# Two pairs by seven products between plain ones in the FFN's first GEMM, and another order of splits at query projection and attention

## The chip, the core and the metric

The kernel runs on one core of one Trainium2 chip. The metric is the device time of one execution in microseconds. The time of the kernel before is 2525.53 us, the median of 3 runs (2525.16 to 2525.58).

## The reference

A decoder trunk of two layers on 1024 tokens with 16 learned tokens ahead of them (1040 columns), width 1024, in float32. Layer 0 is a Mamba-2 mixer and an FFN. Layer 1 is grouped-query attention in a window of 128 tokens, with a sink logit for each head, and an FFN. What matters here is the FFN, and query projection and attention:

```python
def conv_ffn(hn, w_up, conv_w, conv_b, w_down):
    u = causal_dwconv(hn @ w_up, conv_w, conv_b)      # (1040, 2 * 2816), 3 taps
    gate, val = u[..., :D_FF], u[..., D_FF:]
    return (jax.nn.silu(gate) * val) @ w_down

q = (hn @ w_q).reshape(bsz, seq_len, N_KV_HEADS, Q_PER_KV, ATTN_HEAD_DIM) * scale
p = softmax(concatenate([s_meta, s_band, s_sink], -1))
return concatenate([om, ob], axis=1) @ w_o
```

## The kernel before

Activations lie with features on the partitions and the 1040 columns (blocks of 272, 384 and 384) along the free side. Each float32 operand of a GEMM is split in two float16 parts, high and low, and a product is three matmuls: high by high, high by low, low by high. Weights come from memory by SyncE's queue into `stage` (two slots of one unit, a 128 x 1024 slice), in the order of the units: a unit is loaded when the low half of the unit two before it has been made (`w_lo`). ScalarE makes the high half (`hi`, `split_hi`, L884), VectorE the low half (`lo`, `split_lo`, L1594). Each engine works through a list of its own in program order and waits on semaphores.

**The FFN's first GEMM** (`ffn_up` of each engine) goes through 22 pairs, gate tile and value tile i. A plain pair is two tiles of 3 blocks x 8 k x 3 matmuls, 144 in all. ScalarE takes each tile from PSUM to `UB` and makes the first tap of the convolution, VectorE the other two (`conv_tile`, L2094), ScalarE the gate's SiLU (L1412), VectorE the product of both (`product`, L2102), ScalarE the high part of the hidden tile (L1416) and GpSimd its low part (`hidden_lo`, L791).

From pair 7 on every second pair, 8 of the 15 pairs 7 to 21, is computed by seven products of half-size blocks in place of eight (`seven_pair`, a Strassen-Winograd scheme): tokens, k and the two tiles are each cut in two. The seven weight operands are A11, A12, A22 as loaded and the sums S1 to S4, made from `stage` by GpSimd (`weight_sums`, L803 to L810; S3 and S4 overwrite parts of `stage`, S1 and S2 use one buffer `tmp`). ScalarE makes the seven high halves (`op_high`, L1356), VectorE the low ones (`op_low`, L2026), in one set of buffers `OPS`. They stand in the plain pair ahead: four before its first convolution, three before its second. The low half of S4 is the last to read `stage`; with it `w_lo` counts two, and the loads of the next pair go out. TensorE (L2659 to L2661) multiplies in the order A11, S2, A12, S3, S1, A22, S4, each in two pieces of 272 and 248 columns (`e + q`, 14 groups of 12 matmuls, PSUM bank `(e + q) % 7`). VectorE adds the products up from PSUM into `UB` (`add`, L2053), counting `seven_v`; group 13 needs the bank that the addition (6, 0) frees. Between the additions it makes the low halves of the next plain pair (`lo_next`), then come the taps (L2042) and the product. TensorE's first matmul is at L2260 to L2262 for plain pairs; those behind a seven-product pair wait for `seven_v` counts (`after_seven`).

**Query projection and attention.** VectorE's list before query projection is `k_low`, `pre(3, block)` for three blocks (normalised input and its low part) and the low halves of the units U_Q to U_Q + 3, in the order U_Q, U_Q + 1, U_Q + 2 (inside `pre` of the second block), U_Q + 3. In the projection it evacuates 24 groups (L2183) and, at some of them, splits the next units up to U_O + 1, the second unit of the output projection. Then it prepares the sinks and runs the attention's chunks n = 0 to 39: `masked(n)` (L2204) after TensorE's `scores(n)`, ScalarE's `exps(n)` (L1539), VectorE's `denominators(n)` (L2211), GpSimd's normalisation (L869), TensorE's transposes (L2776, L2778) and values, and the split of the result (`out_hi` on ScalarE, `out_lo` L2226 on VectorE). The output projection waits for the last `out_lo`.

Of the kernel before, what the change touches and what calls it, by code (L numbers as in the profile page):

```python
# [5 lines left out]
P = 128  # L6
# [19 lines left out]
WS = 64.0  # L26
# [76 lines left out]
NS = (KF - SF + 1) // 2  # L103
HALF, KH = L // 2, KD // 2
A11, A12, A22, S1, S3, S2, S4 = range(7)
# [57 lines left out]
def program(nc, h0, wa, wd, wdt, prm, out):  # L163
# [4 lines left out]
    with ExitStack() as ctx:  # L168
# [74 lines left out]
        tmp = BIG[:, 21, 0:HP]  # L243

        def op_src(o):
            return (stage[:, 1, 0:HP], stage[:, 1, HP:2 * HP], stage[:, 0, HP:2 * HP], tmp, stage[:, 0, 0:HP], tmp,
                    stage[:, 1, HP:2 * HP])[o]

# [407 lines left out]
        def _(eng):  # L656
# [137 lines left out]
            def weight_sums(layer, m, i0, before):  # L794

                n = NS * layer + i0
                a11, a12, a21, a22 = stage[:, 1, 0:HP], stage[:, 1, HP:2 * HP], stage[:, 0, 0:HP], stage[:, 0, HP:2 * HP]
                eng.drain()
                for s_ in range(2):
                    eng.wait_ge(w_in[s_], m * 32 + 16 * ((U_UP[layer] + 2 * (SF + 2 * i0)) // 2 + 1))  # L800
                if n > 0:
                    eng.wait_ge(op_lo, m * 7 + (7 * (n - 1) + 6))
                eng.tensor_tensor(tmp, a21, a22, ALU.add).then_inc(op_sum, 1)  # L803
                eng.drain()
                eng.tensor_tensor(a21, a11, a21, ALU.subtract).then_inc(op_sum, 1)
                before()
                eng.wait_ge(op_lo, m * 7 + (7 * n + 4))
                eng.tensor_tensor(tmp, tmp, a11, ALU.subtract).then_inc(op_sum, 1)
                eng.drain()
                eng.tensor_tensor(a12, a12, tmp, ALU.subtract).then_inc(op_sum, 1)  # L810

            def ffn_up(layer):

                for t in range(SF - 2):
                    hidden_lo(layer, t)
                weight_sums(layer, 0, 0, lambda: hidden_lo(layer, SF - 2))
                hidden_lo(layer, SF - 1)
                with eng.Fori(0, NS - 1) as m:
                    weight_sums(layer, m, 1, lambda: hidden_lo(layer, m * 2 + SF))
                    hidden_lo(layer, m * 2 + (SF + 1))  # L820
                hidden_lo(layer, KF - 1)
# [55 lines left out]
        def _(eng):  # L877
# [466 lines left out]
            def op_high(layer, m, i0, o):  # L1344

                n = NS * layer + i0
                landed = m * 32 + 16 * ((U_UP[layer] + 2 * (SF + 2 * i0)) // 2 + 1)
                if o == A11:
                    eng.wait_ge(w_in[1], landed)
                    if i0 > 0:  # L1350
                        eng.wait_ge(seven, m * 14 + 14 * n)
                if o == A22:
                    eng.wait_ge(w_in[0], landed)
                if o >= S1:
                    eng.wait_ge(op_sum, m * 4 + (4 * n + o - S1 + 1))
# [4 lines left out]
            def up_tap(layer, m, i0, s_):  # L1360

                col = m * 16 + (C_F[layer] + 8 * (SF + 2 * i0) + 4 * s_)
# [4 lines left out]
            def seven_pair(layer, m, i0, c0, gate, hidden, split_next):  # L1367

                n, i = NS * layer + i0, m * 2 + (SF + 2 * i0)
                eng.wait_ge(conv[1], i + c0)  # L1370
                for q in range(2):
                    eng.wait_ge(seven, m * 14 + (14 * n + 1 + q))
                    eng.activation(up_out(layer, 1, q, False), PS[:, q, 0:piece(layer, q)[1]], ACT.Copy,
                                   scale=1.0 / WS).then_inc(seven_a, 1)
                split_next(0)
                split_next(1)
                eng.drain()
                eng.wait_ge(seven_v, m * 14 + (14 * n + 12))
                up_tap(layer, m, i0, 0)
                eng.drain()  # L1380
                eng.wait_ge(seven_v, m * 14 + (14 * n + 14))
                up_tap(layer, m, i0, 1)
                eng.drain()
                eng.sem_inc(evac, 6)
                gate(i)
                hidden(i)

            def ffn_up(layer, boundary_):
# [18 lines left out]
                def split(i, s_, width=KD * P):  # L1407
                    split_hi(i * 16 + units_loaded(u0 + s_ + 2, s_), s_, width)

# [51 lines left out]
                def last_plain(m, i0):  # L1461

                    i = m * 2 + (SF - 1 + 2 * i0)
                    for o in (A11, A12, A22, S1):
# [1429 lines left out]
```

## Time and profile before

| | |
|---|---|
| median of 3 runs | 2525.53 us |
| the profiled execution | 2525.95 us |
| its span, first to last instruction | 2524.2 us |
| mean granted clock of TensorE | 0.992 |
| TensorE, VectorE, ScalarE, GpSimd busy | 98%, 64%, 46%, 24% of the span |
| first GEMM of the FFN, layer 0 and layer 1 | to about 1240 and 2290 us |
| query projection, attention | about 1520 to 1614, 1614 to 1737 us |

Engines in the rows: PE is TensorE (PEld its weight load), DVE VectorE, ACT ScalarE, POOL GpSimd, SP SyncE. A timeline row has start and duration in us, engine and line, operation, output<-input by the program's names, shape and count; in brackets stands the idle time of the engine just before it and what ended it. Matmuls overlap, so their starts tell the pace, and their durations do not.

### The profile page before, as it was taken

The numbers are of one execution on the slowest core, as the hardware profiler recorded it, in microseconds if no ns is written. First come the engines' busy times: TensorE is split into PE (matmuls) and PEld (weight loads), VectorE is DVE, ScalarE is ACT, GpSimd is POOL, SyncE is SP. The second block draws the span as 40 slices with busy tenths as digits, with TensorE's granted clock in tenths as the row PEclk, the third lists the DMA queues.
The fourth block names the chain that finished last, engine by engine and source line by source line (L and its number), as shares of the span: only waits on it lengthen the run. The fifth ranks groups of instructions, "written<-read, shape, count | busy, mean of one in ns | idle before, by whom it ended". The sixth has DMA issues, their size and how long they took to land.

```text
span 2524.2 us, 45974 instructions
## 1 busy us (share of the span) xinstructions
PE 2470.5 (98%) x18254; PEld 1724.5 (68%) x18254; DVE 1615.6 (64%) x2424; ACT 1155.4 (46%) x2166; POOL 602.3 (24%) x417
## 2 busy tenths in 40 slices
PE   8999999999999999999999999899999999999998
PEld 5566666666665667777766666676656777777665
DVE  6676777787868887777511276594379777772123
ACT  5455655666415554444311255595355444441111
POOL 1002113122142122232122113264411223221221
PEclk9999999999999999999999999999999999999999
DMA  3132222323132111212311112100121121213111
GB/s 118 54 104 79 85 84 80 97 68 99 45 127 101 51 51 50 65 35 66 126 46 58 40 34 68 34 2 18 43 110 50 51 66 34 66 56 126 46 57 67
DMA packets 67808, 167.69 MB, mean 66 GB/s; under 512 B 5680, under 2 KB 37840, under 8 KB 67408
## 3 DMA queue, kind: packets, MB, share of 16 engines
q1 hardware_dynamic: 67664, 165.70, 19.8%
q8 instruction: 99, 1.62, 0.3%
q14 instruction: 45, 0.37, 0.0%
HBM read 151.76 MB, written 12.86 MB: 65 GB/s over the span
## 4 chain that ended last, share of the span: by engine, by line
PE 86%; DVE 8%; ACT 3%; ACTq 1%; POOL 1%; issue 1%; DVEq 1%; DMA 0%
PE PS L2260 22%; PE PS L2262 22%; PE PS L2261 22%; PE PS L2661 4%; PE PS L2659 4%; PE PS L2660 4%; PE PS L2536 1%; PE PS L2543 1%; DVE BIG L1629 1%; PE PS L2525 1%; DVE TT L1693 1%; POOL BIG L869 1%; PE PS L2354 1%; ACT BIG L1539 1%; DVE R L460 1%
## 5 line engine op out<-in xcount | busy, mean ns | idle before, releaser
L2260 PE MATMUL PS<-R,whi 128*128 128x384 f16 (+2 forms) x2400 | 747.4, 311 | 2.6 <-DVE wlo L1594 1.6
L2262 PE MATMUL PS<-R,wlo 128*128 128x384 f16 (+2 forms) x2400 | 747.2, 311 | 0.0
L2261 PE MATMUL PS<-R,whi 128*128 128x384 f16 (+2 forms) x2400 | 747.1, 311 | 0.0
L1594 DVE SCALAR_TENSOR_TENSOR wlo<-stage,whi 128x1024 f16<-128x1024 f32 (+1 forms) x148 | 204.5, 1383 | 380.7 <-ACT whi L884 379.9
L2260 PE MATMUL PS<-BIG,whi 128*128 128x384 f16 (+2 forms) x1404 | 435.4, 310 | 4.9 <-DVE wlo L1594 4.2
L2262 PE MATMUL PS<-BIG,wlo 128*128 128x384 f16 (+2 forms) x1404 | 435.4, 310 | 0.0
L2261 PE MATMUL PS<-BIG,whi 128*128 128x384 f16 (+2 forms) x1404 | 435.3, 310 | 0.0
L2260 PEld LDWEIGHTS PS<-R,whi 128*128 128x128 f16 x2400 | 235.3, 98 | 127.7 <-issue 14.2
L2261 PEld LDWEIGHTS PS<-R,whi 128*128 128x128 f16 x2400 | 235.4, 98 | 121.3 <-issue 9.8
L2262 PEld LDWEIGHTS PS<-R,wlo 128*128 128x128 f16 x2400 | 235.4, 98 | 118.0 <-issue 1.0
L884 ACT ACTIVATE whi<-stage 128x1024 f16<-128x1024 f32 (+1 forms) x148 | 162.5, 1111 | 148.3 <-PE PS L2262 128.5
L791 POOL TENSOR_TENSOR BIG<-TT,BIG 128x1040 f32 (+3 forms) x44 | 95.4, 2168 | 462.4 <-ACT BIG L1416 462.4
L2094 DVE SCALAR_TENSOR_TENSOR TT<-UB,pr,TT 128x1040 f32<-128x1040 f32 (+1 forms) x104 | 161.6, 1554 | 59.6 <-ACT TT L1421 46.8
L2260 PEld LDWEIGHTS PS<-BIG,whi 128*128 128x128 f16 x1404 | 137.2, 98 | 76.4 <-issue 6.5
L2261 PEld LDWEIGHTS PS<-BIG,whi 128*128 128x128 f16 x1404 | 137.2, 98 | 68.7 <-issue 2.6
L2262 PEld LDWEIGHTS PS<-BIG,wlo 128*128 128x128 f16 x1404 | 137.2, 98 | 68.0
L748 POOL TENSOR_TENSOR TT<-R 128x384 f32<-128x384 f32 (+2 forms) x63 | 51.5, 832 | 400.6 <-ACT R L897 261.6
L2659 PE MATMUL PS<-hT,AUX 128*128 128x272 f16 (+3 forms) x512 | 140.1, 274 | 0.0
L2661 PE MATMUL PS<-hT,AUX 128*128 128x272 f16 (+3 forms) x512 | 140.0, 274 | 0.0
L2660 PE MATMUL PS<-hT,AUX 128*128 128x272 f16 (+3 forms) x512 | 139.9, 273 | 0.0
L1693 DVE SCALAR_TENSOR_TENSOR TT<-UB,pr,TT 128x1040 f32<-128x1040 f32 x72 | 102.4, 1422 | 46.9 <-ACT TT L994 42.9
L1416 ACT ACTIVATE BIG<-TT 128x1040 f32 (+3 forms) x44 | 46.8, 1064 | 180.2 <-DVE TT L2102 180.2
(285 smaller groups left out, 4556.7 us busy)
## 6 DMA issues: line engine op xcount, KB each, us to landing
stage<-wa SPq DMA_DIRECT2D x164, 512.0 KB, 3.5
stage<-wd SPq DMA_DIRECT2D x32, 704.0 KB, 4.0
TT<-cs_rows SPq DMA_DIRECT2D x32, 512.0 KB, 3.7
h_keep<-hT SPq DMA_DIRECT2D x2, 4160.0 KB, 12.4
EC<-cs_rows SPq DMA_DIRECT2D x64, 128.0 KB, 3.7
hT<-h SPq DMA_DIRECT2D x4, 1536.0 KB, 10.6
hT<-h_keep SPq DMA_DIRECT2D x4, 1536.0 KB, 8.5
out<-hT SPq DMA_DIRECT2D x4, 768.0 KB, 3.5
```

Of the source, the lines that this page charges most:

```text
L748: eng.tensor_tensor(T1[:, s:s + n], cut(mix(m, b), b, lo_), cut(mix(m, b), b, lo_), ALU.mult)
L791: eng.tensor_tensor(BIGh[:, ds(t, 1), L + a:2 * L], T2[:, a:], BIGh[:, ds(t, 1), a:L], ALU.subtract).then_inc(hid_lo, 1)
L884: eng.activation(WH[slot + 2 * aux][:, 0:width], stage[:, slot, 0:width], ACT.Copy, scale=WS).then_inc(w_hi, 1)
L1594: eng.scalar_tensor_tensor(out=WL[d][:, 0:width], in0=stage[:, slot, 0:width], scalar=WS, in1=WH[d][:, 0:width], op0=ALU.mult, op1=ALU.sub ...
L1693: r = eng.scalar_tensor_tensor(out=T0, in0=UB[:, i % 2, o:o + L], scalar=prc(C_AW + (g * GT + j) * CONV_A + k), in1=T0, op0=ALU.mult, op1= ...
L2094: r = eng.scalar_tensor_tensor(out=dst, in0=cin[:, o + ld_:o + L], scalar=prc(col + k), in1=dst, op0=ALU.mult, op1=ALU.add)
L2260: eng.matmul(acc, WH[slot][:, ws], xh, start=first, stop=False)
L2261: eng.matmul(acc, WH[slot][:, ws], xl, start=False, stop=False)
L2262: return eng.matmul(acc, WL[slot][:, ws], xh, start=False, stop=last)
L2659: eng.matmul(acc, ops[o][:, w], moving(0, kk, q), start=(kk == 0), stop=False)
L2660: eng.matmul(acc, ops[o][:, w], moving(1, kk, q), start=False, stop=False)
L2661: r = eng.matmul(acc, ops[7 + o][:, w], moving(0, kk, q), start=False, stop=(kk == KH - 1))
```

## The change

The stretch from pair 7 on gets another pattern: a seven-product pair 7, then four turns of one plain pair and two seven-product pairs (8, 9, 10; 11, 12, 13; 14, 15, 16; 17, 18, 19), then plain 20 and seven-product 21. That makes 10 seven-product pairs in place of 8. The operands are numbered in TensorE's order, S2 gets a buffer of its own (`tmp2`). The operands of the second of two adjacent pairs are made inside the first: ScalarE's high halves ahead of its taps, S4's between them; VectorE's low halves A11, S2, A12, S3 between the additions and S1 behind the taps; A22 and S4 inside the second pair itself. ScalarE's copies of a pair's first product (`seven_first`) move ahead of the hidden tile of the pair before. At query projection the low halves of U_Q + 1 to U_Q + 3 and the high halves of U_Q + 2 and U_Q + 3 move ahead of `pre` and `split_x` of the second block; the sinks are prepared ahead of the projection's evacuations; `masked(0)` moves ahead of the last evacuation; the halves of U_O + 1 move from the end of the projection to the third last chunk of attention.

```diff
-NS = (KF - SF + 1) // 2
+RS = 2
+RP = RS + 1
+NR = (KF - SF - 3) // RP
+NS = 2 + RS * NR
-A11, A12, A22, S1, S3, S2, S4 = range(7)
+A11, S2, A12, S3, S1, A22, S4 = range(7)
+FIRST, REST = (A11, S2, A12, S3), (S1, A22, S4)
...
@@ GpSimd: weight_sums @@
                 eng.tensor_tensor(tmp, a21, a22, ALU.add).then_inc(op_sum, 1)
                 eng.drain()
+                eng.tensor_tensor(tmp2, tmp, a11, ALU.subtract).then_inc(op_sum, 1)
                 eng.tensor_tensor(a21, a11, a21, ALU.subtract).then_inc(op_sum, 1)
+                eng.drain()
                 before()
-                eng.wait_ge(op_lo, m * 7 + (7 * n + 4))
-                eng.tensor_tensor(tmp, tmp, a11, ALU.subtract).then_inc(op_sum, 1)
-                eng.drain()
-                eng.tensor_tensor(a12, a12, tmp, ALU.subtract).then_inc(op_sum, 1)
+                eng.wait_ge(op_lo, m * (7 * RS) + (7 * n + A12 + 1))
+                eng.tensor_tensor(a12, a12, tmp2, ALU.subtract).then_inc(op_sum, 1)
...
@@ ScalarE: op_high, seven_pair @@
+                if beside:
+                    eng.wait_ge(seven, m * (14 * RS) + (14 * (n - 1) + 2 * o + 2))
...
+                if op_next is not None:
+                    for o in FIRST + REST[:-1]:
+                        op_next(o)
                 eng.drain()
+                eng.wait_ge(seven_v, m * (14 * RS) + (14 * n + 12))
+                up_tap(layer, m, i, 0)
+                if op_next is not None:
+                    op_next(S4)
...
-                gate(i)
-                hidden(i)
+                gate(i_)
+                if op_next is not None:
+                    seven_first(layer, m, i + 1, n0 + 1, c0)
+                hidden(i_)
...
@@ VectorE: seven_pair @@
                     add(2, q, u2[q], c11[q])
+                if op_own is not None:
+                    op_own(A22)
                 eng.drain()
                 for q in range(2):
                     add(4, q, c11[q], c11[q])
-                lo_next(0)
+                if op_own is not None:
+                    op_own(S4)
+                if lo_next is not None:
+                    lo_next(0)
+                ops(A11, S2)
                 for q in range(2):
                     add(6, q, u3[q], u2[q])
-                lo_next(1)
+                if lo_next is not None:
+                    lo_next(1)
+                ops(A12, S3)
                 for q in range(2):
                     add(8, q, u4[q], u2[q])
...
+                ops(S1)
+                product(m * RP + i)
...
@@ VectorE: ffn_up @@
-                with eng.Fori(0, NS - 1) as m:
-                    seven_pair(layer, m, 0, product, lambda s_: split_lo(m * 4 + (u0 + 2 * SF + 3 + s_), s_))
-                    last_plain(m, 1)
+                with eng.Fori(0, NR) as m:
+                    last_plain(m, SF + 1, 1, SF)
+                    for j in range(RS - 1):
+                        seven_pair(layer, m, SF + 2 + j, 1 + j, product, op_next=lambda o: op_low(layer, m, 2 + j, o),
+                                   op_own=(lambda o: op_low(layer, m, 1 + j, o)) if j else None)
+                    seven_pair(layer, m, SF + RP, RS, product, lo_plain(m, SF + RP + 1),
+                               op_own=lambda o: op_low(layer, m, RS, o))
...
@@ VectorE: query projection and attention @@
             pre(3, ORD[0], lambda: lo(U_Q, aux=True))
+            lo(U_Q + 1, aux=True)
             k_low(ORD[2])
-            lo(U_Q + 1, aux=True)
-            pre(3, ORD[1], lambda: lo(U_Q + 2))
+            lo(U_Q + 2)
             lo(U_Q + 3)
+            pre(3, ORD[1])
             pre(3, ORD[2])
...
+                if c == len(Q_SEQ) - 1:
+                    masked(0)
...
+                if q_next(i, b) and i < KD - 1:
+                    lo(U_Q + i + 2)
...
                 if n + 2 < NQD:
                     masked(n + 2)
+                if n + 3 == NQD:
+                    lo(U_O + 1)
...
@@ TensorE: seven_pair @@
+                def free(bank):
+                    if behind_seven:
+                        eng.wait_ge(seven_v, m * (14 * RS) + (14 * (n - 1) + (6, 10, 12, 12, 12, 13)[bank]))
+                    else:
+                        eng.wait_ge(evac, m * (6 * RP) + (kept + bank + 1))
...
+                if behind_seven:
+                    eng.wait_ge(seven_v, m * (14 * RS) + 14 * n)
```

## Rows read from the trace of the kernel before

**Rows 1.** the page: busy us of each engine, share of the span, instructions:

```profile
PE 2470.5 (98%) x18254; PEld 1724.5 (68%) x18254; DVE 1615.6 (64%) x2424; ACT 1155.4 (46%) x2166; POOL 602.3 (24%) x417
```

**Rows 2.** TensorE's waits: us in total, times, longest:

```profile
PE PS L2760 <- DVE small L2204: 4.6, 2, 4.4
```

**Rows 3.** windows, layer 0: busy us of PE, PEld, DVE, ACT, POOL, then clock:

```profile
1040.00:1080.00 40.00, 40.00 (x316) 30.60 (x314) 29.34 (x34) 18.11 (x26) 11.03 (x6) 1.00 0.16 52
```

**Rows 4.** TensorE's timeline (start, us): seven products begin, end, next ones begin:

```profile
1056.80 0.28 PE L2659 MATMUL PS<-R,AUX 128*128 128x272 f16 x1
...
1075.42 0.28 PE L2260 MATMUL PS<-R,whi 128*128 128x272 f16 x1
...
1096.58 0.28 PE L2659 MATMUL PS<-R,AUX 128*128 128x272 f16 x1
```

**Rows 5.** VectorE's timeline in that stage:

```profile
1045.78 2.43 DVE L2026 SCALAR_TENSOR_TENSOR AUX<-stage,AUX 128x512 f16<-128x512 f32 x1 [1.76 <-ACT AUX L1356]
...
1050.32 2.14 DVE L2094 SCALAR_TENSOR_TENSOR TT<-UB,pr,TT 128x1040 f32<-128x1040 f32 x1 [0.30 <-issue]
...
1055.82 0.68 DVE L2026 SCALAR_TENSOR_TENSOR AUX<-stage,AUX 128x512 f16<-128x512 f32 x1
...
1066.60 1.42 DVE L1594 SCALAR_TENSOR_TENSOR wlo<-stage,whi 128x1024 f16<-128x1024 f32 x1
1068.62 1.21 DVE L1594 SCALAR_TENSOR_TENSOR wlo<-stage,whi 128x1024 f16<-128x1024 f32 x1
...
1077.55 1.70 DVE L2042 SCALAR_TENSOR_TENSOR TT<-UB,pr,TT 128x1040 f32<-128x1040 f32 x1 [0.20 <-issue]
...
1082.46 1.24 DVE L2102 TENSOR_TENSOR TT<-TT 128x1040 f32<-128x1040 f32 x1 [0.23 <-issue]
```

**Rows 6.** ScalarE's timeline: two high halves of the next plain pair:

```profile
1065.00 2.00 ACT L884 ACTIVATE whi<-stage 128x1024 f16<-128x1024 f32 x2
```

**Rows 7.** GpSimd's timeline in that stage:

```profile
1045.51 2.16 POOL L791 TENSOR_TENSOR BIG<-TT,BIG 128x1040 f32 x1 [7.04 <-ACT BIG L1416]
...
1051.53 2.07 POOL L810 TENSOR_TENSOR stage<-stage,BIG 128x512 f32<-128x512 f32 x1 [0.16 <-issue]
```

**Rows 8.** SyncE's timeline, then loads of 1054 to 1078, us to landing:

```profile
1056.72 0.86 SPq L613 DMA_DIRECT2D stage<-wa  x2
...
stage<-wa SPq DMA_DIRECT2D x4, 512.0 KB, 4.0
```

**Rows 9.** a wait of TensorE, then windows behind it, columns as Rows 3:

```profile
PE PS L2556 <- DVE BIG L1707: 4.1, 1, 4.1
...
107.00:108.00 1.00, 0.00 (x0) 0.00 (x0) 1.00 (x2) 1.00 (x5) 0.00 (x0) 0.50 0.00 0
...
113.00:114.00 1.00, 1.00 (x7) 0.43 (x6) 0.08 (x1) 0.45 (x1) 0.00 (x0) 0.72 0.01 4
```

**Rows 10.** VectorE's timeline before and at query projection:

```profile
1530.75 1.21 DVE L1594 SCALAR_TENSOR_TENSOR wlo<-stage,whi 128x1024 f16<-128x1024 f32 x1
...
1535.68 1.23 DVE L1594 SCALAR_TENSOR_TENSOR wlo<-stage,whi 128x1024 f16<-128x1024 f32 x1 [0.39 <-ACT whi L884]
...
1543.93 5.74 DVE L2183 SCALAR_TENSOR_TENSOR BIG<-PS,BIG 64x384 f16<-64x384 f32 x10 [0.34 <-ACT BIG L1526]
```

**Rows 11.** timelines of VectorE and TensorE at the start of attention:

```profile
1616.29 1.23 DVE L1594 SCALAR_TENSOR_TENSOR wlo<-stage,whi 128x1024 f16<-128x1024 f32 x1
...
1619.38 0.35 PE L2760 MATMUL PS<-BIG 128*112 128x128 f16 x1 [4.41 <-DVE small L2204]
```

**Rows 12.** timelines at attention's end: ScalarE, VectorE, TensorE twice:

```profile
1730.62 0.19 ACT L1539 ACTIVATION_READ_ACCUMULATOR BIG<-BIG,small 32x1 f32 x1
...
1728.60 0.17 DVE L2211 RECIPROCAL small<-small 32x4 f32<-32x4 f32 x1
...
1732.40 0.31 PE L2776 MATMUL PS<-ident,BIG 32*128 32x32 f32 x1 [0.57 <-POOL BIG L869]
...
1737.45 0.40 PE L2260 MATMUL PS<-R,whi 128*128 128x260 f16 x1 [0.98 <-DVE R L2226]
```

More of the change, by code:

```diff
@@ L792, in hidden_lo, with weight_sums @@
                                   ALU.subtract).then_inc(hid_lo, 1)
[L794 to L796 removed]
+            def weight_sums(layer, m, i, n, before):
+                n += NS * layer
                 a11, a12, a21, a22 = stage[:, 1, 0:HP], stage[:, 1, HP:2 * HP], stage[:, 0, 0:HP], stage[:, 0, HP:2 * HP]
@@ L1565, in _ @@
                     exps(n + 2)
+                if n + 3 == NQD:
+                    hi(U_O + 1)
                 if n > 0:
@@ L2045, in up_taps, with seven_pair @@
                     r.then_inc(conv[s_], 1)
-            def seven_pair(layer, m, i0, product, lo_next):
-                n, i = NS * layer + i0, m * 2 + (SF + 2 * i0)
+            def seven_pair(layer, m, i, n, product, lo_next=None, op_next=None, op_own=None):
+                n0, n = n, NS * layer + n
                 def add(e, q, dst, term):
-                    eng.wait_ge(seven, m * 14 + (14 * n + e + q + 1))
+                    eng.wait_ge(seven, m * (14 * RS) + (14 * n + e + q + 1))
                     eng.scalar_tensor_tensor(out=dst, in0=PS[:, (e + q) % 7, 0:piece(layer, q)[1]],
@@ L2055, in add, with ops @@
                                              op0=ALU.mult, op1=ALU.add).then_inc(seven_v, 1)
+                def ops(*os):
+                    if op_next is not None:
+                        for o in os:
+                            op_next(o)
                 c11, c12 = ([up_out(layer, 1, q, r) for q in range(2)] for r in (False, True))
@@ L2227, in out_lo @@
                 r.then_inc(out_lo_ready, 1)
-            masked(0)
+            for c, (i, b) in enumerate(Q_SEQ):
+                s, n = BLK[b]
+                if c == len(Q_SEQ) - 1:
+                    masked(0)
+                eng.wait_ge(kq_hi, 6 + c + 1)
+                for hh in range(2):
+                    own, other = slice(64 * hh, 64 * hh + 64), slice(64 - 64 * hh, 128 - 64 * hh)
+                    q_ = q_stack(2 * i + hh, s, s + n)
+                    r = eng.scalar_tensor_tensor(out=q_[other], in0=PS[own, c % 6, 0:n],
+                                                 scalar=1.0 / (WS * AD ** 0.5), in1=q_[own],
+                                                 op0=ALU.mult, op1=ALU.subtract)
+                r.then_inc(evac, 1)
+                if q_next(i, b) and i < KD - 1:
+                    lo(U_Q + i + 2)
             masked(1)
```

209 lines of the change are left out of this document (108 added, 101 removed).

## The prediction

> **What bounds the kernel now.** I read the profile in this order: the busy line [rows 1], the waits of TensorE [rows 2], one of the two stages of the FFN's first GEMM by windows [rows 3], then one settled loop pass of that GEMM engine by engine [rows 4 to 8], and last the three places around query projection and attention [rows 9 to 12]. TensorE is busy for 98% of the span, and in the FFN stage a window of 40 us holds 40.00 us of matmuls at full clock [rows 3]. The other layer's stage looks the same, and no wait of TensorE in either is listed. So there only fewer columns help. The reader is to see two things more. VectorE works 29.3 of the 40 us there [rows 3], which looks like a quarter in reserve; but it and ScalarE hand the same tile to and fro, so the reserve is made of waits. And the profiled run took 2525.95 us, its span 2524.2; the median of the runs is 2525.53, so I add differences of spans to the median.
>
> **FFN, what is saved.** A pair by seven products starts at 1056.80 and ends at 1075.42: 18.62 us. The plain pair behind it ends at 1096.58: 21.16 us [rows 4]. Before there are 8 of the 15 pairs behind pair 6 by seven products, afterwards 10 (7, then 9 and 10, 12 and 13, 15 and 16, 18 and 19, then 21). Two pairs a layer: 2 x 2.54 = 5.1 us, for both layers 10.2 us, if TensorE never waits.
>
> **FFN, what is added: a load behind the second pair.** Call the two adjacent pairs A and B. The plain pair P behind B can be loaded into `stage` only when the last low half of B (S4) has been made, because S4 is read from `stage`. Before, S4 was made in the plain pair ahead, its last low ended at 1056.5 [rows 5], the loads went out at 1056.72 [rows 8] while A began, and P's low halves were made at 1066.60 and 1068.62 [rows 5], long before 1075.42. In the new order VectorE makes S4 of B inside B, and the very next item in its queue is the low half of P (`lo_next(0)`). So VectorE stands still for load, ScalarE's high half and its own low half, and behind it in the queue are the additions of products 6 to 13, with the one (6,0) that frees the bank of TensorE's last product but for it. Its length: issue 0.2, landing 4.4 (4.0 is the median of four such loads [rows 8], and of two that go out together the second is the later one), high half 1.0 [rows 6], hand-over 0.2: 5.8 us idle (its lower bound, with a load of 3.5, is 4.9). Then 1.14 low and 0.4 addition: 7.5 us from S4's end to TensorE's go.
>
> TensorE reaches that wait 17.3 us into B (18.62 less the last 1.3). No stall therefore needs S4 of B at B + 9.8. When can it be there? With a VectorE that is never late A's product of gate and value starts 25.7 us into A, as at 1082.46, and takes 1.24 [rows 5]. With low S1 (0.6) and the first part of B (two additions, A22, two additions, S4: 3.0) that is A + 30.5, or B + 11.9; one port wait (below) of 0.6 makes it B + 12.5. 12.5 + 7.5 - 17.3 = 2.7, and I take 3.0 us of stall for the first of the four turns of each layer.
>
> **FFN, how the lag grows.** In the later turns VectorE starts late, since it lost those 5.8 us. I add up its queue over one turn P, A, B, in the order of the changed code: idle for the load 5.8; two low halves of P and the additions of B 6.4; idle for a tap 1.2; taps, last addition and product of B 7.5; idle for ScalarE (hidden tile, then A11's high half) 1.8, the idle time at 1045.78 [rows 5]; seven low halves of 0.61, two tile convolutions of 2 x 1.30, two idles for taps (0.5 and 2.1) and a product: 13.8; A's additions and four lows of B 8.1; idle for a tap 1.2; taps 6.3, S1 0.6, product 1.3; B's first part 3.0. Sum 57.0 us. TensorE's own turn is 21.16 + 2 x 18.62 = 58.4 us. So far VectorE would just keep up.
>
> What decides is the port between VectorE and GpSimd. A low half of 512 columns takes 0.68 us [rows 5], but the one issued at 1045.78 took 2.43: GpSimd's subtraction ran until 1047.67, and it ended 0.5 us behind that [rows 5, 7]. GpSimd's sum of 512 columns at 1051.53 took 2.07 us beside a tap, others of its shape 1.3, so it goes both ways. The additions from PSUM are not touched. In the pass from 1040 to 1080 VectorE loses 4.2 us so: 1.75 at 1045.78, 0.84 and 0.75 at the taps of 1050.32 (2.14 for 1.30) and behind it, 0.2 at 1066.60 (1.42 for 1.21), 0.2 and 0.4 at the taps before and at 1077.55 (1.70) [rows 5]. GpSimd ran six instructions then, 11.0 us [rows 3]. A turn of the new order has eleven of them (three hidden tiles, eight sums), 20 us. By proportion that is 7.6 us; laid beside VectorE's queue one by one I get 8.3 (A11 of A 1.6, S2 of B 2.0, S4 of B 1.0, six taps and products about 3.7). I take 8.3: a turn of 65.3 us. The bounds are 0 and 11 us. The Trainium skill ("SBUF — State Buffer", section "SBUF: two separate sides") says that this pair of ports is an exclusive lock, which a VectorE instruction with two SBUF inputs and a GpSimd one hold for their whole length; the trace agrees, with 2.43 us for 0.68. If the loss were a shared bandwidth instead, the sum would be nearer the 57.0.
>
> Per layer: layer 0: 3.0 + 3 x (65.3 - 58.4) = 23.7, less 5.1: +18.6 us. In layer 1 TensorE's tiles are 13 columns shorter and its turn 57.65 us: 3.3 + 3 x 7.65 - 5.05 = +21.2. Together **+39.8 us**. Moving ScalarE's copies of the first product ahead of the hidden tile gains VectorE 1.6 us at the start of A; that is in the sum. The first GEMM's other pairs and the second GEMM keep their order.
>
> **TensorE's clock.** After a wait of 4.1 us that began at 104.6, the granted clock was at 0.50 (1.2 GHz of 2.4) and came back only at about 113.3, 4.7 us of work later [rows 9]. Stalls of 5 us before B's last product can do the same: 2.3 us of TensorE time each. As VectorE is the later one in P anyway, I count 0 for them and keep 6 x 2.3 = 14 us for the range.
>
> **Query projection.** TensorE waits 4.5 us in all for low halves of units U_Q+1 to U_Q+3 (the last two made at 1530.75 and 1535.68 [rows 10]). Moved ahead, they are ready at 1523.7, 1526.7 and 1529.9 (the last waits for its load, issued at 1523.9, and its high half), so these waits go. But the two `pre` end 1.6 us later, and the first evacuation, which ran at 1543.93, comes at 1545.6 to 1546.8. The seventh group would now start at 1543.8 and needs that bank. So 3.0 of 4.5 us come back: gain 1.8 us (ends 0 and 4.5).
>
> **Start of attention.** TensorE waits 4.4 us for `masked(0)` [rows 2], behind an evacuation, the low half of U_O+1 (1616.29, 1.23 us) and the sinks [rows 11]. With `masked(0)` ahead of the last evacuation it ends at 1615.9 instead of 1619.3; the chain of scores, exponentials and normalisation that follows it is then bound by ScalarE and by GpSimd's copies of queries, about 0.4 us later than by the masking itself: gain 2.9 us (ends 0 and 4.4).
>
> **End of attention.** The high half of U_O+1 now stands behind ScalarE's last exponentials, which end at 1730.8 [rows 12], and its low half in VectorE's queue ahead of `denominators` of the last chunk but one. That reciprocal ran at 1728.60; it now waits until 1731.9 for the high half and 1.2 for the low one, to 1733.1. The last chunk's transposes, at 1732.40 before, start at 1736.0: 3.6 us later, and the output projection (1737.45) with them [rows 12]. Net of both: +0.7. Outside the FFN the sum is -1.1 us (from -7 to +4).
>
> Total: 39.8 - 1.1 = 38.7, so 2525.5 + 38.7 = **2564 us**.
>
> **Rivals.**
> 1. *The port costs little and VectorE keeps up.* For it: its queue sums to 57.0 against 58.4. Then only the load behind S4 counts, 0.4 to 3 us a turn, eight turns: -10.2 + 3 to 24 - 1 = -8 to +13, that is 2517 to 2539. It decides from a port loss under 1.4 us a turn. Against it is the row of 2.43 us, and that a turn has eight sums where a pass before had four.
> 2. *All is hidden.* S4 lands by B + 9.8 and the full 10.2 + 1 is gained: 2514 us, the other side. It needs VectorE 3 us quicker in a chain whose links all have rows; a ScalarE that runs taps earlier could do part of it.
> 3. *The stalls also halve the clock and TensorE becomes the late one in P.* Up to +14: 2570 to 2585. For it [rows 9], against it that VectorE has more to do in P than TensorE.
> 4. *The reordering beside attention goes wrong or the FFN does not change at all:* not likely, as the code is plain; part of the ranges.
>
> **How the numbers follow.** Forecast (turn of 62 to 67 us) 0.74; rival 1 0.12, of which a third is faster, a third about the same; rival 3 0.08; rival 2 0.06. About 0.2%, 5 us, is what a measurement here can tell from none. Slower: 0.74 + 0.08 + 0.04 = 0.86; same 0.04; faster 0.10. The range goes from the top of rival 1 to the upper end of rival 3: 2536 to 2584. The forecast alone spans 2548 to 2575.
>
> **What would show it.** TensorE's waits in the FFN: rows on VectorE's addition of `UB` of 3 us in the first turn and about 5 in the later ones, at the last group of each second pair; VectorE idle 5.8 us for `whi` once a turn; period of three pairs near 65 us; low halves of 2 us and more where GpSimd runs. In attention: the wait of 4.4 us gone, the last transposes later. I would be wrong if S4 of B ends before B + 10, or if those loads land in 3 us.

## The result and the profile after

The changed kernel takes 2563.1 us (median, 2559.5 to 2564.0) against 2525.6 us before: ratio 1.0143, 95% interval 1.0131 to 1.0156, 37.5 us slower. The profiled execution took 2562.72 us with a span of 2560.6; the span grew by 36.4 us, and the comparison below goes by spans. Forecast were 38.7.

The page's busy line (columns as [rows 1]) and TensorE's waits (as [rows 2]) of the kernel after:

```profile
PE 2478.6 (97%) x18350; PEld 1742.0 (68%) x18350; DVE 1658.1 (65%) x2500; ACT 1162.9 (45%) x2170; POOL 643.6 (25%) x433
...
PE PS L2727 <- DVE UB L2087: 26.3, 8, 4.1
...
PE PS L2850 <- POOL BIG L880: 8.0, 8, 5.0
...
PE PS L2321 <- DVE BIG L2283: 3.1, 1, 3.1
PE PS L2834 <- DVE small L2250: 3.0, 2, 2.0
```

No engine's share has moved by more than a point, yet a new row stands on top: a wait of 3.3 us on average, eight times, of a seven-product matmul (L2727) for VectorE's addition (L2087). In place of the wait of 4.4 us for the first mask [rows 2] stand two, of 1.0 and 2.0 us (last row); the last three rows are the places around attention, of which more below.

By the starts of TensorE's first matmul of each kind (as [rows 4]) the time divides so. From pair 7's start to the end of pair 21 the FFN of layer 0 took 297.08 us before and takes 312.57, that of layer 1 took 293.89 and takes 311.17: +15.5 and +17.3, so **+32.8** in the FFN. The stretch between the two FFN stages grew from 752.4 to 755.5 us, the rest of the span by 0.6: **+3.6** outside.

A turn is now a plain pair P and two seven-product pairs A and B. Its length, from one P to the next, is 61.5, 63.3, 65.1 and 64.0 us in layer 0 and 59.8, 64.9, 62.8 and 64.4 in layer 1; TensorE's own work in it is 58.4 and 57.8. One turn and what ends it, from the timelines of TensorE, VectorE, ScalarE and SyncE (SPq: issue of the loads); start, us, then the instruction, in brackets its idle time before:

```profile
1018.12 0.43 PE L2321 MATMUL PS<-R,whi 128*128 128x272 f16 x1
...
1080.08 0.28 PE L2727 MATMUL PS<-R,AUX 128*128 128x248 f16 x1 [3.83 <-DVE UB L2087]
...
1081.46 0.43 PE L2321 MATMUL PS<-R,whi 128*128 128x272 f16 x1
...
1071.58 2.01 DVE L2060 SCALAR_TENSOR_TENSOR AUX<-stage,AUX 128x512 f16<-128x512 f32 x1
1078.45 1.23 DVE L1629 SCALAR_TENSOR_TENSOR wlo<-stage,whi 128x1024 f16<-128x1024 f32 x1 [4.86 <-ACT whi L895]
1079.59 0.76 DVE L2087 SCALAR_TENSOR_TENSOR UB<-PS,UB 128x272 f32<-128x272 f32 x2
...
1077.36 1.06 ACT L895 ACTIVATE whi<-stage 128x1024 f16<-128x1024 f32 x1 [6.69 <-DMA stage<-wa]
...
1073.81 8.17 SPq L621 DMA_DIRECT2D stage<-wa  x4
```

Read it in the order of time: S4's low half (L2060) ends at 1073.59, the load is issued at 1073.81 and lands by 1077.36, the high half takes 1.06, VectorE has stood idle for 4.86 us, makes the low half (L1629), and only then comes the addition for which TensorE waits until 1080.08. In the kernel before the first of these low halves was made 8.8 us before the end of the seven-product pair, which takes 18.6 [rows 4, 5].

### The profile page after: what moved, and what is told of

It is laid out like the page before. It is cut to its first block, busy times and chain, and to the rows that moved or that the text cites. A ratio compares the mean times of both kernels' runs of the same rounds, so it can differ in the third digit from the quotient of the medians.

```text
span 2560.6 us, 46249 instructions
## 1 busy us (share of the span) xinstructions
PE 2478.6 (97%) x18350; PEld 1742.0 (68%) x18350; DVE 1658.1 (65%) x2500; ACT 1162.9 (45%) x2170; POOL 643.6 (25%) x433
## 4 chain that ended last, share of the span: by engine, by line
PE 72%; DVE 12%; DVEq 5%; ACT 4%; issue 3%; DMA 2%; POOL 1%; ACTq 1%; POOLq 0%; SPq 0%
PE PS L2321 19%; PE PS L2322 19%; PE PS L2323 19%; DMA stage<-wa 2%; DVE TT L2076 2%; PE PS L2727 2%; PE PS L2729 2%; PE PS L2728 2%; PE PS L2597 1%; PE PS L2604 1%; DVEq L2063 1%; DVE BIG L1664 1%; PE PS L2586 1%; DVE UB L2087 1%; DVE TT L1728 1%
## 5 line engine op out<-in xcount | busy, mean ns | idle before, releaser
L2321 PE MATMUL PS<-R,whi 128*128 128x384 f16 (+2 forms) x2208 | 690.3, 313 | 2.7 <-DVE wlo L1629 1.5
L2322 PE MATMUL PS<-R,whi 128*128 128x384 f16 (+2 forms) x2208 | 689.8, 312 | 0.0
L2323 PE MATMUL PS<-R,wlo 128*128 128x384 f16 (+2 forms) x2208 | 689.2, 312 | 0.0
L1629 DVE SCALAR_TENSOR_TENSOR wlo<-stage,whi 128x1024 f16<-128x1024 f32 (+1 forms) x140 | 193.4, 1383 | 423.3 <-ACT whi L895 422.5
L2321 PEld LDWEIGHTS PS<-R,whi 128*128 128x128 f16 x2208 | 218.2, 99 | 120.0 <-issue 14.4
L2322 PEld LDWEIGHTS PS<-R,whi 128*128 128x128 f16 x2208 | 218.0, 99 | 113.3 <-issue 9.6
L2323 PEld LDWEIGHTS PS<-R,wlo 128*128 128x128 f16 x2208 | 218.0, 99 | 109.7 <-issue 1.0
L895 ACT ACTIVATE whi<-stage 128x1024 f16<-128x1024 f32 (+1 forms) x140 | 155.5, 1115 | 208.8 <-PE PS L2323 129.7
L2727 PE MATMUL PS<-hT,AUX 128*128 128x272 f16 (+3 forms) x640 | 174.9, 273 | 1.2 <-ACT UB L1385 1.2
L2729 PE MATMUL PS<-hT,AUX 128*128 128x272 f16 (+3 forms) x640 | 174.7, 273 | 0.0
L2728 PE MATMUL PS<-hT,AUX 128*128 128x272 f16 (+3 forms) x640 | 174.6, 273 | 0.0
L2727 PE MATMUL PS<-R,AUX 128*128 128x272 f16 (+1 forms) x480 | 134.0, 279 | 26.3 <-DVE UB L2087 26.3
L2142 DVE SCALAR_TENSOR_TENSOR TT<-UB,pr,TT 128x1040 f32<-128x1040 f32 (+1 forms) x88 | 123.0, 1398 | 43.5 <-ACT TT L1448 33.1
L2076 DVE SCALAR_TENSOR_TENSOR TT<-UB,pr,TT 128x1040 f32<-128x1040 f32 (+1 forms) x80 | 122.4, 1531 | 33.4 <-ACT TT L1376 24.1
```

Of the source, the lines that this page charges most:

```text
L895: eng.activation(WH[slot + 2 * aux][:, 0:width], stage[:, slot, 0:width], ACT.Copy, scale=WS).then_inc(w_hi, 1)
L1629: eng.scalar_tensor_tensor(out=WL[d][:, 0:width], in0=stage[:, slot, 0:width], scalar=WS, in1=WH[d][:, 0:width], op0=ALU.mult, op1=ALU.sub ...
L2076: r = eng.scalar_tensor_tensor(out=dst, in0=UB[:, s_, o + a:o + L], scalar=prc(col + k), in1=dst, op0=ALU.mult, op1=ALU.add)
L2142: r = eng.scalar_tensor_tensor(out=dst, in0=cin[:, o + ld_:o + L], scalar=prc(col + k), in1=dst, op0=ALU.mult, op1=ALU.add)
L2321: eng.matmul(acc, WH[slot][:, ws], xh, start=first, stop=False)
L2322: eng.matmul(acc, WH[slot][:, ws], xl, start=False, stop=False)
```

## The experiments

**The parts apart.** The FFN's part alone (query projection and attention as before), and the other part alone (FFN as before). Of the first edit the core is shown, the second is its mirror:

```diff
# FFN alone: the order at projection and attention as before
-            lo(U_Q + 2)
-            lo(U_Q + 3)
-            pre(3, ORD[1])
+            pre(3, ORD[1], lambda: lo(U_Q + 2))
+            lo(U_Q + 3)
...
-                if n + 3 == NQD:
-                    lo(U_O + 1)
```

> The change without its parts at query projection and attention. By the traces of before and after, the stretch from pair 7 to pair 21 is 15.5 us longer in layer 0 and 17.3 us in layer 1, and the rest of the span 3.6 us longer. If the parts are independent: 2525.5 + 32.8 = 2558 to 2560 us, with TensorE's waits on additions of 2 to 4 us at the last product but for one group of each second pair. If the order at attention had fed back on layer 1's FFN, the 17.3 us of layer 1 would change.

> The other half of the change alone, the FFN as before. Theory: query projection loses 1.3 us (4.5 us of waits go, a wait of 3.1 comes for the seventh group's bank, and the granted clock falls to 0.50 behind it), the start of attention gains 2.7, its end loses 4.5: 3 us longer, 2528 to 2529 us. As predicted, without a fall of the clock, it would be 2524.5.

Measured: 2559.8 us (ratio 1.0133, interval 1.0116 to 1.0150) and 2528.0 us (1.0010, 1.0000 to 1.0019). The first has the eight waits on the addition, 26.8 us in all, and its two FFN stages take 312.3 and 311.8 us; the second has the FFN of before and its stretch between the stages is 2.6 us longer. So the FFN brings 34 of the 37.5 us. The other orders cost some 2 us rather than gain, a difference that only just clears the noise.

**One pair by seven products instead of two.** The changed kernel with its constant at one, and the single pair's low halves all made in the plain pair ahead:

```diff
-RS = 2
+RS = 1
...
-                               op_own=lambda o: op_low(layer, m, RS, o))
+                               op_own=(lambda o: op_low(layer, m, RS, o)) if RS > 1 else None)
```

> The whole change with its constant of two pairs set to one, so that pairs by seven products and plain pairs alternate one by one again, as in the kernel before, while the rest of the change (numbering, the other order of splits at query projection and attention) stands. Theory (only the second pair in a row has its load behind S4 in VectorE's queue): the FFN is that of the kernel before, and the time that of the kernel with the other order of splits alone, 2527 to 2530 us. Rival, something else in the new helper costs by itself: over 2535 us.

Measured: 2528.2 us (1.0007, 0.9997 to 1.0016), the same as the other orders alone. Neither the numbering of operands nor the helper costs by itself; it takes two adjacent pairs.

**VectorE's queue: the low halves of P later.** In pair B the two low halves of P, with the idle time ahead of them, are moved behind the additions for which TensorE waits:

```diff
                 if op_own is not None:
                     op_own(S4)
-                if lo_next is not None:
+                if lo_next is not None and op_own is None:
                     lo_next(0)
...
-                if lo_next is not None:
+                if lo_next is not None and op_own is None:
                     lo_next(1)
...
+                if lo_next is not None and op_own is not None:
+                    lo_next(0)
+                    lo_next(1)
                 add(12, 0, c12[0], u4[0])
```

> The changed kernel, but in the second pair of a turn VectorE makes the two low halves of the next plain pair behind the additions of products 8 to 11, so that no addition stands behind the load. Theory (VectorE's queue standing still for the load makes the wait and the lag): the waits on additions go, a wait of 2 to 3 us for the plain pair's low halves comes in their place at its start, both layers together some 20 us shorter, about 2541 us (2534 to 2548). Rival (VectorE has too much work in a turn, whatever its order, with GpSimd at its port): the time stays at 2558 to 2563 us.

**The other end of the same chain: A22 and S4 of B earlier**, between the taps of A's two tiles, so that `stage` is free earlier and the load is nearly done when VectorE asks for it (the line with `op_own(A22)` goes as well):

```diff
                 up_taps(layer, m, i, n0, 0, (0,))
+                ops(S1, A22, S4)
                 up_taps(layer, m, i, n0, 1, (1, 0))
-                ops(S1)
                 product(m * RP + i)
...
-                if op_own is not None:
-                    op_own(S4)
```

> The changed kernel, but VectorE makes the low halves S1, A22 and S4 of the second pair inside the first one, between the taps of its two tiles. The load of the plain pair then goes out some 10 us earlier, about 4 us into the second pair. Theory (S4's late low half and the load behind it): no wait at the last product but one; a wait of up to 3 us stays in the middle of the second pair for ScalarE's copies of its first product, as VectorE's taps come later. 25 to 35 us shorter, about 2531 us (2526 to 2538). Rival (too much work on VectorE and its port): at most a few us shorter, 2555 or more.

Measured: 2526.8 us (1.0007, 0.9997 to 1.0016) and 2526.6 us (1.0004, 0.9995 to 1.0014): either move takes back the whole loss. For the first that is more than expected: 2541 us, from 2534 to 2548, stood there, with a wait of 2 to 3 us on P's low halves, and about 1 us was left of it. The same low half with the idle time before it, from VectorE's timelines, first with the low halves later, then with S4 earlier:

```profile
1074.45 2.42 DVE L1629 SCALAR_TENSOR_TENSOR wlo<-stage,whi 128x1024 f16<-128x1024 f32 x2 [1.38 <-ACT whi L895]
```

```profile
1066.74 2.48 DVE L1629 SCALAR_TENSOR_TENSOR wlo<-stage,whi 128x1024 f16<-128x1024 f32 x1 [0.58 <-ACT whi L895]
```

The idle time of 4.86 us shrinks to 1.38 and 0.58, and no row on the additions is left. In layer 0 a turn is 59.0 to 60.0 us in the one and 58.4 to 59.7 in the other. What stays is one wait of about 1 us a turn, on P's low half (10.0 us in 11 waits over the whole kernel) in the first, on ScalarE's copy of B's first product (7.5 in 6) in the second. That is where most of the saving of 10.2 us goes in these two.

**The port.** GpSimd's sums of weights cut to 16 columns. All loads, waits and VectorE's work are kept; the two operands that had stood in `tmp` and `tmp2` are read from `stage` instead. The kernel leaves the sums out for all other columns, so its output is not the reference's:

```diff
-                eng.tensor_tensor(tmp, a21, a22, ALU.add).then_inc(op_sum, 1)
+                eng.tensor_tensor(tmp[:, 0:16], a21[:, 0:16], a22[:, 0:16], ALU.add).then_inc(op_sum, 1)
```

> The whole change, with GpSimd's part of a pair's weight sums cut to 16 of its columns (these sums are left out for all other columns, and products 5 and 6 of a pair take a block of the weights in place of the sum, so the output differs); instruction counts, loads, waits and VectorE's work stay. Theory of the prediction, as the runs so far leave it (the cost is VectorE's idle for the load; the lock of the port adds 8.3 us to VectorE's work in a turn): the idle stays, with the additions after it faster by up to some 2 us a turn; 8 stalls shrink from 3.3 to about 1.5 to 2 us, and less of the half clock follows, so 2543 to 2553 us. Rival, the port is nothing here: 2560 to 2566 us as the change. Rival, the port is all of it: 2526 us or less, and no wait on VectorE's additions left in the pairs.

Measured: 2533.8 us (1.0035, 1.0021 to 1.0048), below the range of the theory and above that of the port as the only cause. The eight stalls came out as expected, 1.5 to 2.0 us (13.9 in all); the range given with them did not follow from them: 2525.5 and 13.9, less the 10.2 saved, plus 2.6 outside the FFN, is 2531.8. Three turns of the changed kernel, then two of this one, columns as [rows 3]:

```profile
1018.12:1081.46 63.34, 59.51 (x483) 47.36 (x481) 48.24 (x58) 27.25 (x38) 21.50 (x11) 0.99 0.13 47
1081.46:1146.54 65.08, 61.31 (x482) 48.19 (x480) 49.82 (x63) 27.26 (x38) 20.82 (x11) 0.95 0.16 53
1146.54:1210.58 64.04, 61.20 (x481) 48.21 (x480) 48.92 (x60) 27.36 (x38) 21.17 (x11) 0.95 0.15 49
```

```profile
1015.38:1075.66 60.28, 58.58 (x483) 46.88 (x480) 45.30 (x60) 27.20 (x38) 10.83 (x11) 1.00 0.16 52
1075.66:1135.78 60.12, 58.58 (x483) 46.89 (x481) 45.29 (x60) 27.20 (x38) 10.64 (x11) 1.00 0.15 52
```

VectorE does the same instructions in 45.3 us instead of 48.2 to 49.8, and the turn falls from 64.2 us on average to 60.2. Its idle time, the turn less the busy time, hardly moves: 15.1 to 15.3 us before this edit and 14.8 to 15.0 with it, and the wait for `whi` is still 4.94 us. So it is VectorE's busy time that GpSimd stretches, not a later operand.

**Both taken away:** S4 early and the short sums together.

> The change with both suspected costs taken away at once: low S1, A22 and S4 of the second pair made inside the first, and GpSimd's sums cut to 16 columns (these sums are left out for all other columns, products 5 and 6 take a block of weights in their place, so the output differs). Theory (each of the two alone leaves VectorE's turn at 59.4 to 60.2 us against TensorE's 58.4): together they leave VectorE some 55 us, no wait of TensorE on VectorE's additions, and the full saving of 10 us in the two stages, less the 2.6 of the other order of splits: 2517 to 2520 us. Rival, the waits on ScalarE's copies come from their place in the queue alone and stay at about 1 us a turn: 2524 to 2527 us.

Measured: 2517.9 us (0.9969, 0.9957 to 0.9981), as the theory has it. No wait of TensorE over 0.2 us is left in the two stages, and they take 292.0 and 288.9 us, which is the sum of their pairs, 10.1 less than before. A turn of it:

```profile
1013.84:1072.24 58.40, 58.40 (x483) 46.97 (x480) 45.21 (x60) 27.09 (x38) 11.80 (x11) 1.00 0.17 55
```

Seen together, the cures do not add up: with the idle time gone the kernel gets 36 us faster than the change, with the sums gone 29, with both gone 45. A turn is 64 us long where TensorE's own work is 58.4; each of the two alone takes the turn to 59 to 60 us, and nothing can be gained below 58.4.

**Projection and attention.** The order of before and the new one mixed: the fourth query unit's low half inside the normalisation of the second block, the first mask early, the halves of the output unit (U_O + 1) behind the last chunk of attention. Once with the FFN of before, once with the FFN whose S4 is early:

```diff
             lo(U_Q + 2)
-            lo(U_Q + 3)
-            pre(3, ORD[1])
+            pre(3, ORD[1], lambda: lo(U_Q + 3))
...
-                if n + 3 == NQD:
-                    lo(U_O + 1)
...
             out_lo(NQD - 1)
+            lo(U_O + 1)
```

> The kernel before's FFN with the same order of splits in between the two at query projection and attention. Theory: waits of 4.5 us at the projection go, of which up to 2.3 come back at the seventh group without a fall of the clock, 2.7 at the start of attention are gained and nothing is lost at its end: 2520 to 2523 us. Rival, the stall at the seventh group stays, with the half clock behind it: 2526 to 2529 us.

> FFN as in the run with the second pair's low S1, A22 and S4 made inside the first pair (2526.6), and an order of splits at query projection and attention in between the two: the fourth query unit's low half inside the normalisation of the second block, its high halves around that unit, the first mask early as in the change, and the second unit of the output projection last, as before the change. Theory: in the run with the other order of splits alone, a wait of 3.1 us at the seventh group and the half clock behind it cost 6 us, and the end of attention 2; with the low half earlier inside the block's normalisation and the output unit put back, the gains of 1.8 to 2.9 at projection and 2.7 at the start of attention stand: 2519 to 2523 us. Rival, the stall at the seventh group stays, with its half clock: 2526 to 2529 us.

Measured: 2519.5 us (0.9972, 0.9963 to 0.9981) and 2518.7 us (0.9970, 0.9957 to 0.9982), both about half a microsecond or less below the ranges given. TensorE's waits tell why. Its timeline with this order and the FFN of before:

```profile
1547.83 0.34 PE L2263 MATMUL PS<-BIG,whi 128*128 128x384 f16 x1 [0.36 <-DVE BIG L2226]
```

The seventh group waits 0.36 us instead of 3.12, and the clock behind it stays at 1.00. At the start of attention the waits for the masks are 1.0 and 2.0 us, as in the change. The last two waits of the transposes for GpSimd are 0.7 and 0.4 us, where the changed kernel has one of 5.0, and the stretch between the FFN stages is 745.8 us, 6.6 less than before.

**A version that beats both.** On top of that low S1, A22 and S4 of B go behind A's last taps, so that ScalarE's copies for B start earlier, and P's low halves one step later:

```diff
-                ops(S1, A22, S4)
                 up_taps(layer, m, i, n0, 1, (1, 0))
+                ops(S1, A22, S4)
...
                 for q in range(2):
                     add(6, q, u3[q], u2[q])
+                if lo_next is not None and op_own is not None:
+                    lo_next(0)
...
                 for q in range(2):
                     add(8, q, u4[q], u2[q])
+                if lo_next is not None and op_own is not None:
+                    lo_next(1)
```

> The version with both mendings (2518.7 us) with two moves in the second pair: its low S1, A22 and S4 come behind the last taps of the first pair instead of between them, so that ScalarE's copies for the second pair start 2 us earlier, and the two low halves of the plain pair come one step later in VectorE's queue, behind the additions of products 6 and 7 and of 8 and 9. Theory: the waits of 0.8 to 1.5 us on ScalarE's copies, one a turn, are what eats most of the 10 us that two more pairs by seven products save; they go, and VectorE still finds its next high half ready to within 1 us: 2510 to 2515 us. Rival, VectorE with the port has no slack left for 58.4 us a turn whatever the order, and the waits only move to another row: 2517 to 2521 us.

Measured: **2512.7 us** (0.9947, 0.9933 to 0.9960), 12.8 us faster than before and 50 faster than the change. Its waits in the seven-product lines, and one turn:

```profile
PE PS L2725 <- DVE UB L2087: 1.1, 3, 0.4
...
PE PS L2725 <- ACT UB L1385: 0.3, 1, 0.3
...
1013.16:1071.56 58.40, 58.40 (x483) 46.91 (x480) 47.22 (x59) 27.31 (x38) 21.08 (x11) 1.00 0.16 53
```

With GpSimd's full 21.1 us of work in the turn VectorE gets by with 47.2 us, and TensorE is the bound again. The two stages take 292.9 and 290.4 us, which is 7.7 of the 10.2 us saved. So the port alone does not undo the change; it did so through an order that had no room for it. Which of the two moves brings how much was not run apart.

## Why the prediction was right, step by step

The mechanism in the FFN was right, and so was the size within a fifth. That the total came out within 1.2 us of the forecast is in part luck: the FFN was forecast 7.0 us too long (39.8 against 32.8) and the rest 4.7 us too short (-1.1 against +3.6), and the two misses nearly cancel.

**The saving.** 18.62 and 21.16 us for the two kinds of pair stand; the run without waits shows 10.1 of the 10.2 us.

**The load behind S4.** Right in kind and place, a little too long. Forecast were 5.8 us of idle VectorE, with 4.9 as the lower bound; 4.86 was measured, because the load landed in 3.55 us rather than the 4.4 taken from the median and a surcharge for the second of two. From S4's end to TensorE's go: 6.5 instead of 7.5 us. In the first turn S4's low half ended 13.1 us into B (forecast 12.5), and the stall was 2.1 us (2.7, rounded to 3.0).

**VectorE's turn.** Forecast 57.0 us of queue and 8.3 lost at the port, 65.3; measured 64.2 in layer 0 (63.3, 65.1, 64.0). The groups of VectorE's instructions over three turns (1018 to 1210; line, shapes, count, busy us, mean ns, idle before) let both terms be read:

```profile
L2076 DVE SCALAR_TENSOR_TENSOR TT<-UB,pr,TT 128x1040 f32<-128x1040 f32 x24 | 37.0, 1540 | 11.5 <-ACT TT L1376 8.3 <-issue 3.1
L2060 DVE SCALAR_TENSOR_TENSOR AUX<-stage,AUX 128x512 f16<-128x512 f32 x30 | 34.9, 1188 | 5.8 <-ACT AUX L1368 5.8
L2087 DVE SCALAR_TENSOR_TENSOR UB<-PS,UB 128x272 f32<-128x272 f32 x42 | 18.3, 435 | 2.5 <-issue 1.3 <-PE PS L2729 0.7
...
L2142 DVE SCALAR_TENSOR_TENSOR TT<-UB,pr,TT 128x1040 f32<-128x1040 f32 x12 | 17.4, 1448 | 8.0 <-ACT TT L1448 5.9 <-issue 2.1
...
L2060 DVE SCALAR_TENSOR_TENSOR AUX<-BIG,AUX 128x512 f16<-128x512 f32 x12 | 10.7, 894 | 0.4
L1629 DVE SCALAR_TENSOR_TENSOR wlo<-stage,whi 128x1024 f16<-128x1024 f32 x6 | 7.3, 1220 | 14.5 <-ACT whi L895 14.5
```

An undisturbed tap takes 1.30 us and a low half 0.68. The 36 taps are 7.6 us over that, the 42 low halves 17.0: 24.6 in three turns, **8.2 us a turn** where 8.3 were forecast. What is left of the turn is 56.0 against 57.0, and 0.9 of that difference is the shorter idle time for the load. One term of the 57.0 was added up wrongly: seven low halves of 0.61, the two convolutions, two idle times and a product make 13.3 us, and 13.8 was written. The additions, which read PSUM, keep their 0.44 us (435 ns), as the sum assumed. With the short sums the taps are back at 1301 ns, and in three turns (1015.38 to 1195.94) the 42 low halves take 41.2 us: 4.2 us of loss a turn, nearly all of it beside GpSimd's three hidden tiles, which were left whole. The Trainium skill ("SBUF — State Buffer", section "SBUF: two separate sides") says that whichever of the two starts first holds the pair of ports for its whole instruction, while the other waits. The rows agree: S4's low half takes 2.01 us where a GpSimd instruction of 2.17 us had begun 0.7 us before it, in one turn after the other.

**The sum over the turns.** Over TensorE's own work the first turn of layer 0 was 3.1 us longer, the other three 17.3 together, the last plain pair 0.2: less 5.1 that is +15.5, against 18.6. In layer 1 it was 2.0 + 18.9 + 1.4 - 5.0 = +17.3, against 21.2. The miss is in the main the 1.1 us a turn just named, and in layer 1 also a first stall that was 1.5 us shorter than taken.

**The clock.** The prediction counted nothing for a halved clock in the FFN, since VectorE is the later one in P. The clock did fall behind the long stalls, as windows of the changed kernel show around a stall of 3.77 us that ends at 1144.09:

```profile
1141.00:1142.00 1.00, 0.00 (x0) 0.00 (x0) 0.00 (x0) 0.64 (x1) 0.00 (x0) 1.00 0.95 389
...
1143.00:1144.00 1.00, 0.00 (x0) 0.00 (x0) 1.00 (x3) 0.66 (x1) 0.00 (x0) 0.50 0.00 0
...
1148.00:1149.00 1.00, 1.00 (x6) 0.66 (x5) 0.47 (x2) 0.70 (x1) 0.00 (x0) 0.50 0.93 348
1149.00:1150.00 1.00, 1.00 (x9) 0.74 (x7) 0.29 (x1) 0.56 (x1) 0.00 (x0) 0.74 0.13 53
```

TensorE loses some 2.7 us by it (5 us at 0.50, 1.2 GHz, and a window at 0.74). Yet the turn is hardly longer for it. In the run with the short sums the clock stayed at 1.00, and VectorE's idle time in a turn was 14.8 to 15.0 us; here it is 15.1 to 15.3, and no more than 0.3 us of it in a turn ends with a matmul. The rest of the difference between the turns, 3.7 of 4.0 us, is VectorE's busy time. So the slow matmuls fill time that would have been a longer stall. That is why the waits read 3.8 us and not the "about 5" that the prediction said a reader would find. Rival 3 saw the fall rightly and its price wrongly. Not covered by VectorE are only the first turn of layer 0 (3.1 us longer with a stall of 2.1, so 1.0) and the last plain pair of each stage (0.2 and 1.4).

**Outside the FFN** the forecast was -1.1, and +3.0 was measured between the stages, +3.6 in all. The step that failed is the projection, forecast as a gain of 1.8 us and measured as a loss of 1.3. Its mechanism held: the waits of 4.5 us went, and the seventh group waited 3.12 us for its bank (3.0 forecast). But this stall halved the clock as well, which the prediction had counted for the FFN's range and not here. Windows of the changed kernel:

```profile
1561.00:1563.00 2.00, 0.00 (x0) 0.00 (x0) 0.85 (x2) 1.93 (x5) 1.55 (x7) 0.88 0.02 8
1563.00:1565.00 2.00, 1.69 (x6) 0.85 (x7) 1.92 (x4) 1.93 (x5) 2.00 (x5) 0.50 0.00 0
1565.00:1567.00 2.00, 2.00 (x8) 0.94 (x7) 1.92 (x4) 1.45 (x4) 2.00 (x4) 0.50 0.00 0
1567.00:1569.00 2.00, 2.00 (x8) 0.91 (x6) 1.94 (x4) 0.00 (x0) 2.00 (x5) 0.50 0.00 0
```

It stays at 0.50 until about 1569, and as no other engine is later there, that costs its full 3 us: at the start of the seventh group the changed kernel had gained 1.7 us on the kernel before since the start of the projection, behind the half clock it had lost 1.3. This price is not a fixed one. The other runs with this order have the same stall, of 3.1 to 3.3 us. In five of them the half clock behind it cost 1.7 us and the projection came out about even, and in the run with both causes taken away the clock stayed at 1.00 and the projection gained 1.5 us. The wait in that run, and a window behind it:

```profile
1541.77 0.34 PE L2317 MATMUL PS<-BIG,whi 128*128 128x384 f16 x1 [3.30 <-DVE BIG L2279]
...
1543.00:1545.00 2.00, 2.00 (x14) 1.19 (x13) 1.94 (x4) 1.89 (x5) 2.00 (x5) 1.00 0.00 0
```

So the forecast holds where the clock does, and it had no term for the clock. The Trainium skill ("TensorE: Matmul & The Clock Gate", section "HAM oscillation — how this bites in real kernels") says that a wait which throttles TensorE makes it start slow again each time. In the two stretches shown from the changed kernel it did start slow (0.50), and what else was late decided whether that cost anything; the run just shown did not start slow behind a wait as long.

The start of attention gained 2.9 us, as forecast. But TensorE's waits there fell by only 1.8 us (from 5.3 to 3.5), and the granted clock was also below full for about half as long, which the prediction had not counted; no run separates the two. The end lost 4.8 us up to the output projection (3.6 forecast): the last chunk but one's reciprocal stands in VectorE's queue behind the low half of U_O + 1, as foreseen, and its transposes come 4.5 us later.

```profile
1746.48 1.23 DVE L1629 SCALAR_TENSOR_TENSOR wlo<-stage,whi 128x1024 f16<-128x1024 f32 x1 [3.44 <-ACT whi L895]
1747.62 0.16 DVE L2257 RECIPROCAL small<-small 32x4 f32<-32x4 f32 x1
...
1749.16 0.31 PE L2850 MATMUL PS<-ident,BIG 32*128 32x32 f32 x1 [4.98 <-POOL BIG L880]
```

**Rivals 1 and 2.** Rival 1 needed a port loss under 1.4 us a turn, and 8.2 was measured. But its band was reached another way: with 4.2 us of loss left, the run with the short sums has turns only 1.8 us too long and takes 2533.8 us. Rival 2, 2514 us, did not happen, but the last version above, reordered in both places, gets there.

## What to carry to other kernels

Where an in-order engine gets a load's consumer as its next item, everything behind it waits for the DMA; put the work that others need ahead of it, or free the buffer one stage sooner. Add up the whole queue of the second-busiest engine over a period, idle times and port losses included, and compare it with the bound's own period: 65% busy over the span did not show that 64 us stood against 58. A cure is worth only what lies above that bound, so two causes that each explain nearly the whole loss are no contradiction.

## What was unexpected of the hardware

The length of a stall alone does not tell whether the clock falls behind it. All eight stalls of the run with the short sums, 1.5 to 2.0 us, left the granted clock at 1.00 in both stages. Behind the first stall of the change, 2.1 us, ended at 1016.00, the clock fell (windows of 1 us, columns as [rows 3]):

```profile
1016.00:1017.00 1.00, 1.00 (x7) 0.83 (x8) 1.00 (x2) 0.00 (x0) 0.00 (x0) 0.70 0.11 33
1017.00:1018.00 1.00, 1.00 (x7) 0.73 (x6) 1.00 (x3) 0.00 (x0) 0.00 (x0) 0.50 0.64 209
1018.00:1019.00 1.00, 1.00 (x6) 0.68 (x5) 0.74 (x3) 0.00 (x0) 0.00 (x0) 0.50 0.69 283
1019.00:1020.00 1.00, 1.00 (x8) 0.71 (x6) 0.91 (x4) 0.00 (x0) 0.00 (x0) 0.60 0.66 139
```

That is 1.7 us of clock missing behind 2.1 us of stall. But in the run of the FFN's part alone a stall of 3.81 us, ended at 1207.70, left the clock at 1.00. And one wait of 2.32 us at the query projection, where the two kernels are alike, had the clock at 1.00 behind it in the kernel before and at half in that run; the wait in each, and a window behind it:

```profile
1532.11 0.32 PE L2260 MATMUL PS<-BIG,whi 128*128 128x384 f16 x1 [2.32 <-DVE wlo L1594]
...
1532.00:1534.00 2.00, 1.89 (x12) 1.20 (x13) 2.00 (x3) 0.52 (x1) 0.73 (x1) 1.00 0.70 190
...
1547.24 0.48 PE L2316 MATMUL PS<-BIG,whi 128*128 128x384 f16 x1 [2.32 <-DVE wlo L1628]
...
1548.00:1550.00 2.00, 2.00 (x8) 0.91 (x6) 1.88 (x5) 1.21 (x3) 0.00 (x0) 0.50 0.88 212
```

So a stall of 2 to 4 us is to be planned with a range: by these traces it costs between its own length and nearly twice that, where nothing else is late.

And VectorE's loss at the port per us of GpSimd's work was nearly the same in three kernels: 4.2 us beside 11.0 before, 8.2 beside 21.2 in a turn of the change, 4.2 beside 10.7 with the short sums, about 0.4 each time. In these kernels the proportion was a good estimate; 7.6 us by it stood in the prediction beside the 8.3 laid out one by one. It is not a constant: in a turn of the fastest version the loss is 6.8 us beside 21.1, a third.
